# Scaling by the norm's root moved behind the first mixer's input projection

## The reference, cut to what matters

```
h    = x * rsqrt(mean(x^2) + eps) * norm_mix[0]      # RMSNorm
proj = h @ w_in_even                                 # 1024 x 2816, fp32
pa, pu, pv = split(proj, [1792, 512, 512])
# pa: token shift, then RWKV-7 time mixing;  gelu(pu), gelu(pv): spatial gating
```

## Time and profile before

| | |
|---|---|
| median of three runs | 1112.14 us (1112.07 to 1114.34) |
| profiled execution, its own time | 1115.32 us |
| its span | 1113.4 us |
| PE busy | 1053.6 us, 95% |
| DVE busy | 812.4 us, 73% |
| ACT busy | 645.0 us, 58% |
| mean granted TensorE clock | 0.977 |

### The profile page before, as it was taken

How to read it: one execution, slowest core, us unless ns; L and a number is a source line. 1 busy time by engine, 2 the same in 40 slices (tenths; PEclk the granted TensorE clock), 3 DMA queues, 4 the chain that set the end, 5 groups by cost and what they waited for, 6 DMA issues and landing times.

```text
span 1113.4 us, 17557 instructions
## 1 busy us (share of the span) xinstructions
PE 1053.6 (95%) x7402; PEld 886.3 (80%) x7402; DVE 812.4 (73%) x904; ACT 645.0 (58%) x657; POOL 20.3 (2%) x23
## 2 busy tenths in 40 slices
PE   8999989999999999999999888879999999999996
PEld 7999889877778888888878856658678888888884
DVE  5357555565778998999967576474668899988993
ACT  4456224424767768677654132654466767777674
POOL 0000000000000000000004000000000000000000
PEclk9999999799999999999999899989999999999998
DMA  8332100126389999999948387655169999999961
GB/s 350 130 115 83 39 4 3 44 81 259 138 318 351 360 356 362 373 352 366 371 143 327 121 330 287 228 190 195 71 250 334 352 358 345 377 358 365 365 238 49
DMA packets 40322, 271.04 MB, mean 243 GB/s; under 512 B 5056, under 2 KB 5520, under 8 KB 9520
## 3 DMA queue, kind: packets, MB, share of 16 engines
q1 hardware_dynamic: 39616, 267.11, 64.2%
q0 software_dynamic: 624, 2.76, 0.6%
HBM read 265.78 MB, written 4.07 MB: 242 GB/s over the span
## 4 chain that ended last, share of the span: by engine, by line
PE 83%; DVE 8%; ACT 3%; DMA 3%; issue 2%; SPq 0%; ACTq 0%; DVEq 0%
PE ps L911 10%; PE ps L913 10%; PE ps L912 10%; PE ps L937 5%; PE ps L939 5%; PE ps L938 5%; PE ps L356 3%; PE ps L357 3%; PE ps L358 3%; PE ps L1748 3%; DMA arena<-in_k_near 2%; DVE w_lo L348 1%; PE ps L949 1%; PE ps L924 1%; ACT w_hi L341 1%
## 5 line engine op out<-in xcount | busy, mean ns | idle before, releaser
L348 DVE TENSOR_TENSOR w_lo<-raw,w_hi 128x2048 fp32r<-128x2048 f32 x76 | 173.9, 2289 | 41.8 <-ACT w_hi L341 41.8
L341 ACT ACTIVATE w_hi<-raw 128x2048 fp32r<-128x2048 f32 x76 | 145.4, 1914 | 98.9 <-PE ps L358 43.9
L348 DVE TENSOR_TENSOR lo_more<-raw_more,hi_more 128x2048 fp32r<-128x2048 f32 x48 | 109.9, 2289 | 19.8 <-ACT hi_more L341 19.8
L348 DVE TENSOR_TENSOR w_lo<-raw_more,w_hi 128x2048 fp32r<-128x2048 f32 x48 | 109.9, 2290 | 14.6 <-ACT w_hi L341 14.5
L348 DVE TENSOR_TENSOR lo_more<-raw,hi_more 128x2048 fp32r<-128x2048 f32 x48 | 110.0, 2291 | 14.0 <-ACT hi_more L341 14.0
L356 PE MATMUL ps<-h_hi,w_hi 128*128 128x320 f32 x320 | 103.3, 323 | 6.3 <-DVE arena L2448 5.5
L341 ACT ACTIVATE hi_more<-raw 128x2048 fp32r<-128x2048 f32 x48 | 91.9, 1915 | 25.5 <-PE ps L913 25.5
L341 ACT ACTIVATE w_hi<-raw_more 128x2048 fp32r<-128x2048 f32 x48 | 92.0, 1917 | 16.4 <-PE ps L939 16.4
L357 PE MATMUL ps<-h_lo,w_hi 128*128 128x320 f32 x320 | 100.9, 315 | 0.0
L358 PE MATMUL ps<-h_hi,w_lo 128*128 128x320 f32 x320 | 100.7, 315 | 0.0
L341 ACT ACTIVATE hi_more<-raw_more 128x2048 fp32r<-128x2048 f32 x48 | 91.9, 1915 | 11.0 <-PE ps L939 9.6
(11 more groups left out here) (508 smaller groups left out, 2324.7 us busy)
## 6 DMA issues: line engine op xcount, KB each, us to landing
raw<-in_stream SPq DMA_DIRECT2D x125, 1024.0 KB, 6.8
raw_more<-in_stream SPq DMA_DIRECT2D x96, 1024.0 KB, 7.0
arena<-in_k_near SPq DMA_DIRECT2D x8, 1024.0 KB, 8.7
arena<-in_v_near SPq DMA_DIRECT2D x8, 1024.0 KB, 7.7
arena<-in_k_far SPq DMA_DIRECT2D x8, 512.0 KB, 5.3
arena<-in_v_far SPq DMA_DIRECT2D x8, 512.0 KB, 4.9
arena<-in_bias_prompt SPq DMA_DIRECT2D x1, 1536.0 KB, 7.7
xt<-in_x SPq DMA_DIRECT2D x2, 640.0 KB, 4.6
```

The costliest lines, as they stand in the source:

```text
L341: eng.activation(hi_slot(W_SLOT[c]), raw_chunk(c), ACT.Copy).then_inc(S("w_hi_made"), 1)
L348: eng.tensor_tensor(lo_slot(W_SLOT[c]), raw_chunk(c), hi_slot(W_SLOT[c]), ALU.subtract).then_inc(S("w_lo_made"), 1)
```

## The change

The first mixer now projects `x * norm_mix0` without the root. ACT writes its high part block by block (`raw_hi`), DVE its low part (`raw_lo`), and tile 0 follows them block by block. The squares, the sum over features (now in bank 5 and behind tile 1 on PE), the root and the reciprocal (kept in a new tensor `rstd_in`) come behind. DVE then multiplies each of the 22 tiles in place in its bank by `rstd_in` (`scaled`, new line 1423), and ACT takes a tile only after that (`in0_scaled` in place of `tile_done`). In DVE's loop `split_lo` now stands ahead of `shift_mix`. Chunk 0 is split by halves. The loads are issued as parameters, first half of x, chunk 0, second half of x, constants, chunk 1. An early root of one column loads ACT's table. Of the `warm` products 32 are left of 65.

```diff
         def mix0_act(eng):
             eng.wait_ge(S("constants_set"), 2)
+            eng.activation(small[:, 327:328], eps_norm, ACT.Sqrt)
+            eng.wait_ge(S("params_loaded"), 16)
+            for k in range(KT):
+                if k % 4 == 0:
+                    eng.wait_ge(S(f"x_loaded{k // 4}"), 16)
+                eng.activation(h_hi[:, k, :], xt[:, k, :], ACT.Identity, bias=zero, scale=par("norm_mix0", k)).then_inc(S("raw_hi"), 1)
+                if k == 3:
+                    split_hi_half(eng, AT_IN0, 0)
+            split_hi_half(eng, AT_IN0, 1)
+            eng.sem_inc(S("w_hi_made"), 1)
             for q in range(4):
-                eng.wait_ge(S(f"x_loaded{q // 2}"), 16)
                 eng.activation(squares(0)[:, 2 * q:2 * q + 2, :], xt[:, 2 * q:2 * q + 2, :], ACT.Square).then_inc(S("norm_sq"), 1)
-            split_hi(eng, AT_IN0)
+            split_hi(eng, AT_IN0 + 1)
             norm_root(eng, 0)
-            split_hi(eng, AT_IN0 + 1)
-            norm_split_hi(eng, 0)
+            eng.sem_inc(S("norm_hi"), 2)
...
             for n, i in enumerate(IN0_ORDER):
-                eng.wait_ge(S("tile_done"), tile(AT_IN0, n))
+                eng.wait_ge(S("in0_scaled"), n + 1)
...
-            split_lo(eng, AT_IN0)
-            norm_dve(eng, 0, "norm_mix0", True)
+            for k in range(KT):
+                eng.wait_ge(S("raw_hi"), k + 1)
+                eng.scalar_tensor_tensor(h_lo[:, k, :], xt[:, k, :], par("norm_mix0", k), h_hi[:, k, :], ALU.mult, ALU.subtract).then_inc(S("raw_lo"), 1)
+                if k == 3:
+                    split_lo_half(eng, AT_IN0, 0)
+            split_lo_half(eng, AT_IN0, 1)
...
             split_lo(eng, AT_IN0 + 1)
+            eng.wait_ge(S("norm_root"), 1)
+            eng.reciprocal(rstd_in[:, :], s_root).then_inc(S("norm_rstd"), 1)
+            eng.wait_ge(S("norm_rstd"), 1)
+
+            def scaled(n):
+                eng.wait_ge(S("tile_done"), tile(AT_IN0, n))
+                eng.tensor_tensor(ps[:, IN0_BANK[n], 0:T], ps[:, IN0_BANK[n], 0:T], rstd_in[:, :], ALU.mult).then_inc(S("in0_scaled"), 1)
+
+            scaled(0)
...
             for n, i in enumerate(IN0_ORDER):
+                if n:
+                    scaled(n)
+                if n % 2 and n // 2 + 2 < IN0_CHUNKS:
+                    split_lo(eng, AT_IN0 + n // 2 + 2)
                 if i < A_TILES:
                     shift_mix(n, i)
-                if n % 2 and n // 2 + 2 < IN0_CHUNKS:
-                    split_lo(eng, AT_IN0 + n // 2 + 2)
...
             warm(26)
-            eng.wait_ge(S("norm_loaded"), 32)
-            norm_pe(eng, 0)
-            warm(12)
-            eng.wait_ge(S("norm_rstd"), 1)
-            warm(3)
-            for k in range(KT):
-                eng.wait_ge(S("norm_h"), k + 1)
-                warm(3)
+            eng.wait_ge(S("raw_hi"), 2)
+            warm(6)
...
                 tile_product(eng, IN0_BANK[n], W_SLOT[c], n % 2, h_hi, h_lo, n == 0).then_inc(S("tile_done"), 1)
-                if n == 0:
+                if n == 1:
+                    eng.wait_ge(S("norm_loaded"), 16)
+                    norm_pe(eng, 0)
                     eng.wait_ge(S("small_loaded"), 16 * 7)
```

More of the change, by code:

```diff
@@ L287, in decoder_layers @@
         state = sb("state", [P, HT, 64])
+        rstd_in = sb("rstd_in", [P, T])
         w_end = small[:, 330:378].rearrange("p (a b) -> p a b", a=HT)
@@ L341, in split_hi, with split_hi_half, split_lo_half @@
             eng.activation(hi_slot(W_SLOT[c]), raw_chunk(c), ACT.Copy).then_inc(S("w_hi_made"), 1)
+        def split_hi_half(eng, c, n):
+            cols = slice(CHUNK_ELEMS // 2 * n, CHUNK_ELEMS // 2 * (n + 1))
+            eng.wait_ge(S(f"raw_loaded{RAW_SLOT[c]}"), 16 * RAW_LOADS[c])
+            eng.activation(hi_slot(W_SLOT[c])[:, cols], raw_chunk(c)[:, cols], ACT.Copy).then_inc(S("first_hi"), 1)
+        def split_lo_half(eng, c, n):
+            cols = slice(CHUNK_ELEMS // 2 * n, CHUNK_ELEMS // 2 * (n + 1))
+            eng.wait_ge(S("first_hi"), n + 1)
+            eng.tensor_tensor(lo_slot(W_SLOT[c])[:, cols], raw_chunk(c)[:, cols], hi_slot(W_SLOT[c])[:, cols], ALU.subtract).then_inc(S("first_lo"), 1)
         def split_lo(eng, c):
@@ L353, in tile_product @@
             for k in range(KT):
-                if follow and k % 4 == 0:
-                    eng.wait_ge(S("norm_lo"), k // 4 + 1)
+                if follow:
+                    eng.wait_ge(S("raw_lo"), k + 1)
                 eng.matmul(ps[:, bank, 0:T], hi[:, m, k, :], x_hi[:, k, :], start=(k == 0), stop=False)
@@ L359, in tile_product @@
             return mm
+        NORM_BANK = (5, 0, 2, 0, 0)
         def squares(i):
@@ L380, in norm_root @@
             eng.wait_ge(S("norm_ms"), i + 1)
-            eng.activation(s_root, ps[:, 2 if i == 2 else 0, 0:T], ACT.Sqrt, bias=eps_norm, scale=1.0 / D).then_inc(S("norm_root"), 1)
+            eng.activation(s_root, ps[:, NORM_BANK[i], 0:T], ACT.Sqrt, bias=eps_norm, scale=1.0 / D).then_inc(S("norm_root"), 1)
         def norm_split_hi(eng, i):
@@ L391, in norm_pe @@
                     eng.wait_ge(S("norm_sq"), 4 * i + k // 2 + 1)
-                mm = eng.matmul(ps[:, 2 if i == 2 else 0, 0:T], ones, squares(i)[:, k, :], start=(k == 0), stop=(k == KT - 1))
+                mm = eng.matmul(ps[:, NORM_BANK[i], 0:T], ones, squares(i)[:, k, :], start=(k == 0), stop=(k == KT - 1))
             mm.then_inc(S("norm_ms"), 1)
@@ L1384, in mix0_dve @@
             eng.tensor_scalar(key_left, params[:, key_at:key_at + HT], -1.0, 1.0, ALU.mult, ALU.add).then_inc(S("mix0_vector"), 1)
-            split_lo(eng, AT_IN0)
-            norm_dve(eng, 0, "norm_mix0", True)
-            split_lo(eng, AT_IN0 + 1)
+            for k in range(KT):
[4 more added lines that the diff above has]
+            split_lo_half(eng, AT_IN0, 1)
+            eng.wait_ge(S("first_lo"), 2)
+            eng.sem_inc(S("w_lo_made"), 1)
+            for name, n in (("norm_h", KT), ("norm_lo", 2)):
+                eng.sem_inc(S(name), n)
+            split_lo(eng, AT_IN0 + 1)
+            eng.wait_ge(S("norm_root"), 1)
[5 more added lines that the diff above has]
+            scaled(0)
             eng.wait_ge(S("small_loaded"), 16 * 7)
@@ L1635, in mix0_pe @@
                 c = AT_IN0 + n // 2
-                if n % 2 == 0:
+                if n < 2:
+                    eng.wait_ge(S("first_lo"), n + 1)
+                elif n % 2 == 0:
                     eng.wait_ge(S("w_lo_made"), c + 1)
@@ L2425, in mix1_dve @@
             for k in range(KT):
-                eng.wait_ge(S("raw_hi"), k + 1)
+                eng.wait_ge(S("raw_hi"), KT + k + 1)
                 eng.scalar_tensor_tensor(h_lo[:, k, :], xt[:, k, :], par("norm_mix1", k), h_hi[:, k, :], ALU.mult, ALU.subtract).then_inc(S("raw_lo"), 1)
@@ L2699, in first_tiles @@
                 for k in range(KT):
-                    eng.wait_ge(S("raw_lo"), k + 1)
+                    eng.wait_ge(S("raw_lo"), KT + k + 1)
                     for m in range(2):
@@ L2914, in _ @@
         def _(eng):
+            eng.dma_start(params[:, :], ins["params"]).then_inc(S("params_loaded"), 16)
             for q in range(2):
                 eng.dma_start(xt[:, 4 * q:4 * q + 4, :], ins["x"][:, 4 * q:4 * q + 4, :]).then_inc(S(f"x_loaded{q}"), 16)
+                if q == 0:
+                    load_chunk(eng, 0)
             eng.dma_start(consts[:, 0:2 * P], ins["consts"][:, 0:2 * P]).then_inc(S("norm_loaded"), 16)
-            eng.dma_start(params[:, :], ins["params"]).then_inc(S("norm_loaded"), 16)
-            for c in range(2):
-                load_chunk(eng, c)
+            load_chunk(eng, 1)
             for to, name in ((router[:, :, :, :], "router"), (shift0, "shift0"), (lora, "lora"), (sw, "sgu_w"), (sw8, "sgu_w8")):
```

1 line of the change is left out of this document (removed).

## The result

| | kernel before | changed kernel |
|---|---|---|
| median of the runs (lowest to highest) | 1113.24 us (1112.07 to 1117.04, 4 runs) | 1135.59 us (1132.85 to 1137.38, 4 runs) |
| profiled execution: time, span, mean granted clock | 1115.32 us, 1113.4 us, 0.977 | 1136.33 us, 1134.5 us, 0.965 |
| recurrence starts | 126.58 us | 149.52 us |

The change makes the kernel slower: the medians differ by 22.35 us, where 12.1 were forecast. The ratio on record is 1.0168, 95% interval 1.0133 to 1.0203; the two medians alone stand at 1.0201. So a loss of 22 us is at the upper end of the interval. The page after, in the form of the earlier trace rows: PE works 8 us longer in a span 21 us longer.

What follows compares the result with a forecast made beforehand. Up to the recurrence it took a chain of head work, then PE, with DVE's list nearly full, as the bound. DVE chain +6.7 plus clock 5.4 gave +12.1 on 1112.1: 1124.2 us, range 1121 to 1131.

Steps and rivals of the forecast that it cites:

- tile 7 done to `prep_sums`: DVE and ACT chain from 48.3 to 69.7 us, leaving 1.5 us of the 6.3 gained.
- tile 13 done to `gated`: One chain over DVE and ACT of 25.5 us instead of 19.8, so 5.7 us lost.
- `gated` to `bonus_sums`: DVE's list behind `gated`: 10.1 us instead of 8.1, 2.0 lost, plus 1.1 for the clock.
- The head: a gain of 6.3 us: From the start to tile 7: done at 48.3 instead of 54.60 us, 6.3 us earlier.
- What 22 scalings cost: On DVE: 0.49 us each, 0.40 to the next instruction, 8.8 us together; more cost from where they stand.
- The two waits: PE stands still about 5 us ahead of `prep_sums`, released by ACT's squares, and 4.8 ahead of `gated`, by `vn_rows`.
- The clock: Clock falls to 1.2 GHz behind waits ahead of `prep_sums` (4.3 us) and `gated` (1.1 us): 5.4 us lost.
- sum at constant clock: Start of the recurrence without any clock loss: -1.5 + 5.7 + 2.0 + 0.5 = +6.7 us.
- The clock's upper bound: Clock loss at most 4.3 + 1.1 us and another 3 us in tiles 4, 14 or 18.
- That the clock holds: Rival: same DVE chain without clock loss, +6.7, 1118.8 us; chance 0.27.
- That the gain is kept: Rival: the scalings fit in DVE's idle time ahead of tile 7's mix, 1106.3 us; chance 0.08.
- That tile 4 comes 2 us later: Rival: tile 0 waits for late transfers of x or chunk 0, the head gains less, 1126.2 us; chance 0.07.

Runs made afterwards that it cites:

- later series: The changed kernel itself run and profiled once more on another chip, against the kernel before: 1133.86 us, ratio 1.0150.
- run 3: The kernel before with its 22 tiles multiplied in place by ones on DVE ahead of ACT's take, nothing else changed: 1138.54 us, ratio 1.0192.
- Run 1: The changed kernel with products that nobody reads put into five of PE's waits: 1126.29 us, ratio 1.0081.
- run 2: The changed kernel with DVE's `shift_mix` ahead of `split_lo` again: 1136.81 us, ratio 1.0185.
- run 7: The changed kernel scaling only tiles 0 to 3, later tiles from normalized h, mix ahead of split, two waits filled: 1113.28 us, ratio 0.9967.

## Why the prediction was off

The direction and the mechanism were right, the size was not: the median is 1135.59 us, the forecast 1124.2 with a range to 1131. Two steps failed: the gain of the head, priced 3.8 us too high, and the cost of the clock, priced at 5.4 us where some 14 are found (1.6 of them in the head, and so in both). A part of the distance can be scatter: the four executions of the kernel before that stand beside the first result ran at 1112.07 to 1117.04 us, where 57 others go up to 1123.92, and with the later series' ratio of 1.0150 the median of 1112.1 would become 1128.8, inside the range. But the path was too cheap there as well: the recurrence starts at +22.9 us in the first profile and at +19.6 in the second, against +12.1. The 10.8 us of the first profile by the prediction's steps:

| step | forecast | profile after | too little |
|---|---|---|---|
| tile 0 starts | 10.05 | 10.27 | 0.2 |
| sum over features ends | 19.4 | 23.0 | 3.4 more |
| tile 4 starts | 29.1 | 33.0 | 0.3 more |
| tile 7 done to `prep_sums` | 21.4 us | 21.3 us (52.12 to 73.38) | -0.1 |
| `prep_sums` | 9.65 us | 10.26 us | 0.6 |
| its end to tile 13 done | 8.6 us | 9.9 us (to 93.58) | 1.3 |
| tile 13 done to `gated` | 25.5 us | 25.5 us (to 119.04) | 0.0 |
| `gated` to `bonus_sums` | 10.1 + 1.1 us | 14.75 us | 3.5 |
| `bonus_sums` to the recurrence | 14.0 us | 15.7 us | 1.7 |

(The first three lines come to 3.9; 3.8 are left at tile 7, 52.12 against 48.3.)

- **"The head: a gain of 6.3 us" failed by 3.8.** Two terms. The sum over features was priced at 2.3 us, half of a row that had been "spent waiting for squares". It took 4.06 with nothing to wait for: 16 entries for eight products, two for each, 0.25 us each. The 4.54 of before were nearly all work. And tiles 0 and 1 took 8.67 us, not 7.06, since the clock fell behind the 2.36 us ahead of tile 0. The sum had no term for a fall there; its one row on a wait of that length, the 2.4 us of the earlier trace rows, showed none. In the second profile of the changed kernel there was indeed none at tile 0, and the fall came behind the 2.60 us ahead of tile 4 instead.
- **"What 22 scalings cost" was right.** 0.48 to 0.50 us each, against 0.49 of the earlier trace rows. The two long chains, to `prep_sums` and to `gated`, came out to 0.1 us. That the scalings are what the loss hangs on is shown by run 3, where the scalings alone give 1.0192.
- **The two waits were right:** 4.53 and 4.53 us, released by ACT's squares and by `vn_rows`, as forecast (5 and 4.8).
- **"The clock" was the wrong size: 5.4 us, where 14 are found** (1.6 at tile 0, 4.9 in `prep_sums`, 1.3 in tile 12, 4.6 behind `gated`, 1.7 in and behind `bonus_sums`). The forecast's two places were right. In `prep_sums` 4.9 were lost instead of 4.3. Behind the wait ahead of `gated` 1.1 was taken and 4.6 measured. The forecast's slow stretch was too short, and DVE's list hides next to nothing of it: with that wait filled, `gated` to `bonus_sums` is 10.01 us, against the 10.1 of the sum at constant clock. The other three places were not in the sum. The clock's upper bound (another 3 us "in tiles 4, 14 or 18") was a third of the 8.7 that were missing. Run 1 shows this part: with the waits filled the sum at constant clock, +6.7, becomes +12.4 at the recurrence, and the rest of that is the head (2.3), `prep_sums`, whose fall was put off but not avoided (2.7), and 0.7 between them and `gated`.
- The rule quoted from the Trainium skill ("TensorE: Matmul & The Clock Gate", section "HAM oscillation — how this bites in real kernels"), that the work behind each wait starts at half rate, was used for two waits. The trace agrees behind both, 4.53 us each. The three waits of 2 to 2.6 us are shorter than the several microseconds of the rule, and there the traces are divided: in the first profile the clock fell behind 2.36 (tile 0) and 1.98 us (`bonus_sums`) and not behind 2.60 (tile 4); in the second it fell behind 2.60 and not behind 2.25 and 1.98. Such waits wanted two bounds in the sum, nothing and the full price, and had none.
- **Rivals.** That the clock holds: no. That the gain is kept: no, `prep_sums` starts 2.2 us later than before. That tile 4 comes 2 us later: it came 3.9 later, but for the two reasons above and not for the transfers, which came in time (tile 0 at 10.27).
- The bound of 0.2% between same and slower was of no matter here. The forecast of the order of mix and split, "now ahead of the mix DVE stands idle during `split_hi`", is shown in the waits (4.53 and 4.53 us against 3.09 and 3.8 in run 2), but two series could measure nothing of it in the time.

What stays open: why the clock behind the recurrence is lower in some executions (0.75 to 0.79 from 220 to 260 us) than in others (0.86 to 0.91), even of one kernel, and whether it is the cause of the 4 us or goes with them. No run held that stretch's clock. Open too is why the clock falls behind a given wait of 2 to 2.6 us in one execution and not in the next, and why it falls in the middle of `prep_sums` where no wait stands ahead of it.

## What to carry to other kernels

An operation of half a microsecond on the engine that feeds TensorE costs what it makes wait. Here 22 of them, 9 us of VectorE's time, opened two waits of 4.5 us, which cost as much again in clock. When a change leaves TensorE waiting, price the work behind each wait twice, at 2.4 and at 1.2 GHz. Behind the waits of 4.5 us the lower clock was there in every profile that has them, and 4.9 and 4.6 us were lost; behind those of 2 to 2.6 us it was there in some executions only, 1.5 to 1.7 us each time. The first wait that a new head adds counts too. Put off a normalization only for the tiles that would otherwise wait for it: here scaling four tiles kept the gain, scaling all 22 turned it into a loss.

## What the runs showed of the hardware that was not expected

- Behind waits of 2 to 2.6 us the clock fell in some executions and not in others of the same kernel: behind 2.36 us ahead of tile 0 it was 0.50 in the first profile of the changed kernel. In its second profile it was 1.00 there and 0.95 over the stretch from 30 to 65 us, which holds the 2.6 us wait ahead of tile 4 (tile 4 took 5.15 us instead of 3.63), and 1.00 again behind the 1.98 us ahead of `bonus_sums`. The sum over features started at 18.94 in the one, at 17.51 in the other. PE in the second profile, columns as above:

```profile
9.00:15.00 6.00, 4.86 (x31) 1.00 1.03 407
...
30.00:65.00 35.00, 33.30 (x191) 0.95 0.36 121
...
134.00:140.00 6.00, 6.00 (x41) 1.00 0.00 0
```

- The clock fell during the small products even with no wait ahead of them: with the head alone the last 24 of `prep_sums` took 4.75 us and in run 7 3.88, against 2.78.
- A product of the fp32 sum over features, 320 columns, shows as two entries and 0.5 us at 2.4 GHz, against 0.15 for a product of a tile's split halves.
- Executions of one kernel differ by up to 12 us, nearly all of it with the mean granted clock. What a change does must be read at the end of its own stretch, and its worth in the whole time from many executions.
